# Hymba-style trunk step on one core: weight splits between normed blocks, operand of the output projection rounded in parts, modulation group 35 moved, root table earlier, last stores from two queues

## The reference, cut to what matters

```
mod = silu(c) @ ada_w + ada_b                      # 9 vectors of 2048: shift, scale, gate of three parts
x += 0.5 * g1 * SwiGLU_1(RMSNorm(x) * (1 + s1) + b1)        # 2048 -> 5504 -> 2048
h  = RMSNorm(x) * (1 + s2) + b2
[xb | yb | q | k | v] = h @ w_in                            # 28 blocks of 128 columns
lru = RG-LRU(conv4(xb)) * gelu(yb)                          # 8 heads of 128
att = window attention with sinks(rope(q), rope(k), v)      # 8 q heads, 2 kv heads
x += g2 * ([lru | att] @ w_out)
x += 0.5 * g3 * SwiGLU_2(RMSNorm(x) * (1 + s3) + b3)
y = RMSNorm(x) * norm_final
```

## Time and profile before

| | us |
|---|---|
| median of 3 runs | 2408.03 (2407.75 to 2410.68) |
| profiled execution, its own time | 2407.99 |
| span of its profile | 2405.5 |
| TensorE busy | 2356.3 (98%) |
| VectorE busy | 1202.7 (50%) |
| ScalarE busy | 838.0 (35%) |
| GpSimd busy | 151.1 (6%) |
| mean granted clock of TensorE | 0.995 |

### The profile page before, as it was taken

The page is one execution under the profiler, slowest core; times in us unless marked ns, Lnnn a source line. Parts: engine busy times, 40 slices in busy tenths (PEclk is TensorE's granted clock), DMA queues, the critical chain, the costliest instruction groups (busy, mean ns, idle before and its releaser), DMA issues.

```text
span 2405.5 us, 45693 instructions
## 1 busy us (share of the span) xinstructions
PE 2356.3 (98%) x17264; PEld 2258.3 (94%) x17264; DVE 1202.7 (50%) x2084; ACT 838.0 (35%) x1130; POOL 151.1 (6%) x176
## 2 busy tenths in 40 slices
PE   7999999999999999998999998999999999999998
PEld 3888999999999999998999898999999999999998
DVE  3665434434533454357676746454454454456344
ACT  3332222222222232334566634332333232333234
POOL 3000000000000000021031211000000000000003
PEclk9999999999999999999999999999999999999999
DMA  9999998889889948863444453554554555454553
GB/s 316 359 332 350 281 278 266 263 262 278 270 258 278 270 147 245 255 192 114 146 134 123 123 148 116 147 157 138 154 157 140 149 156 148 140 159 147 145 154 104
DMA packets 680252, 480.98 MB, mean 200 GB/s; under 512 B 15349, under 2 KB 603785, under 8 KB 679801
## 3 DMA queue, kind: packets, MB, share of 16 engines
q1 hardware_dynamic: 678224, 473.36, 65.8%
q0 software_dynamic: 1776, 6.26, 0.8%
q10 hardware_dynamic: 162, 0.14, 0.0%
HBM read 476.53 MB, written 5.13 MB: 200 GB/s over the span
## 4 chain that ended last, share of the span: by engine, by line
PE 91%; DVE 4%; ACT 2%; issue 1%; DMA 1%; DVEq 0%; ACTq 0%
PE ps L558 28%; PE ps L560 28%; PE ps L559 28%; PE ps L569 6%; PE ps L544 1%; DVE lo L1366 1%; DMA ident<-in_identity 0%; ACT hi L1021 0%; DMA mod_raw<-in_ada_w 0%; DVE work L1679 0%; DVE h_lo L1412 0%; DVE work L1725 0%; DVE work L1681 0%; DVE work L1401 0%; DVE work L1427 0%
## 5 line engine op out<-in xcount | busy, mean ns | idle before, releaser
L558 PE MATMUL ps<-h_hi,hi 128*128 128x320 f32 x3456 | 1079.0, 312 | 18.5 <-DVE h_lo L1412 11.8
L560 PE MATMUL ps<-h_hi,lo 128*128 128x320 f32 x3456 | 1070.5, 310 | 0.0
L559 PE MATMUL ps<-h_lo,hi 128*128 128x320 f32 x3456 | 1070.5, 310 | 0.0
L1366 DVE TENSOR_TENSOR lo<-raw,hi 128x1024 fp32r<-128x1024 f32 (+1 forms) x608 | 731.8, 1221 | 492.3 <-ACT hi L1021 491.1
L1021 ACT ACTIVATE hi<-raw 128x1024 fp32r<-128x1024 f32 (+1 forms) x608 | 624.9, 1050 | 1009.6 <-PE ps L560 875.9
L558 PEld LDWEIGHTS ps<-h_hi,hi 128*128 128x128 f32 x3456 | 651.3, 188 | 35.2 <-issue 28.4
L559 PEld LDWEIGHTS ps<-h_lo,hi 128*128 128x128 f32 x3456 | 651.4, 188 | 0.7
L560 PEld LDWEIGHTS ps<-h_hi,lo 128*128 128x128 f32 x3456 | 651.2, 188 | 0.0
L558 PE MATMUL ps<-a_hi,hi 128*128 128x320 f32 x1376 | 426.8, 310 | 1.3 <-DVE a_lo L1540 1.3
L560 PE MATMUL ps<-a_hi,lo 128*128 128x320 f32 x1376 | 425.2, 309 | 0.0
L559 PE MATMUL ps<-a_lo,hi 128*128 128x320 f32 x1376 | 425.1, 309 | 0.0
(11 more groups left out here) (221 smaller groups left out, 875.5 us busy)
## 6 DMA issues: line engine op xcount, KB each, us to landing
raw<-in_ffn_w_gate SPq DMA_DIRECT2D x172, 512.0 KB, 4.2
raw<-in_ffn_w_up SPq DMA_DIRECT2D x172, 512.0 KB, 5.1
raw<-in_ffn_w_down SPq DMA_DIRECT2D x160, 512.0 KB, 4.8
mod_raw<-in_ada_w SPq DMA_DIRECT2D x144, 512.0 KB, 7.8
work<-in_ada_w SPq DMA_DIRECT2D x144, 512.0 KB, 8.2
raw<-in_w_in SPq DMA_DIRECT2D x56, 512.0 KB, 3.8
raw<-in_w_out SPq DMA_DIRECT2D x32, 512.0 KB, 3.8
raw<-in_ffn_w_down SPq DMA_DIRECT2D x16, 384.0 KB, 2.9
```

Source lines behind the costliest of these rows:

```text
L558: mm(out, w_hi, r_hi, start=first, stop=False)
L559: mm(out, w_hi, r_lo, start=False, stop=False)
L560: return mm(out, w_lo, r_hi, start=False, stop=last)
L1366: v.tensor_tensor(lo_slot(u)[:, 0:n], raw_slot(u)[:, 0:n], hi_slot(u)[:, 0:n], ALU.subtract).then_inc(lo_done, 1)
```

## The change

1. `modulate` for the mixer's norm and for the second SwiGLU's norm does the splits of units 4 and 5 itself, ahead of blocks 11 and 13 (`EARLY`); the loops that follow start at their third unit.
2. Group 35: parts 0 and 1 stand between the two matmuls of `sum_of_squares(1)`, parts 2 to 7 behind them; `copy_group(35)` stands between the root and `modulate`, `mod_turn(35)` and `add_mod(35)` behind the mixer's first four projections.
3. `root_table` (the throw-away root) is taken out of `rms`, and out of the program's end, and stands behind the square of block 14.
4. End of the mixer: blocks 0 to 6 are rounded ahead of the last projection's end (`early_operand`), blocks 8 to 11 before the last attention job, 12 to 15 after it; the splits of the output projection's units 4 to 6 stand between what is left of head 7's work.
5. The one store of the last column group that ScalarE's copy feeds is issued from ScalarE's queue (11 stores are left to SyncE).

```diff
+EARLY = (11, 13)
...
+                    if q == 3 and who == "A":
+                        continue
...
                     pe.wait_ge(summed, SUMMED[n] + KB - 1)
                     mm(psum[:, B_NORM, 0:T], ones, sum_sq, start=True, stop=False)
+                    for part in range(first_parts):
+                        mod_unit(part, 35)
                     pe.wait_ge(squared, n * KB + KB)
                     mm(psum[:, B_NORM, 0:T], ones, sq[:, (KB - 1) % 2, :], start=False, stop=True).then_inc(ms_ready, 1)
...
-                    down_eight(u, 0, g, 0, a0 + 4 * CB + TAIL, 35)
+                    down_eight(u, 0, g, 0, a0 + 4 * CB + TAIL, None)
...
-            sum_of_squares(1)
+            sum_of_squares(1, 2)
+            for part in range(2, MODS):
+                mod_unit(part, 35)
...
+                if kv == 0:
+                    pe.wait_ge(mod_done, 36)
...
             four_blocks(U_MIX, (first[0:2], first[2:4]), KB)
+            mod_turn(35)
...
+            def root_table():
+                run(warm, eps, ACT.Sqrt)
+
             def rms(n):
-
-                run(warm, eps, ACT.Sqrt)
...
                 for k in range(first, end):
+                    if u is not None and k in EARLY:
+                        finished(u + EARLY.index(k))
+                        split(u + EARLY.index(k) + SPLIT)
...
+                        if n == KB - 2:
+                            root_table()
...
-            modulate(1, 3, 0, KB)
+            copy_group(35)
+            modulate(1, 3, 0, KB, U_MIX)
...
+            def early_operand():
+
+                act.wait_ge(lru_done, LH - 1)
+                for k in range(LH - 1):
+                    run(h_hi[:, k, :], mix[:, k, :], ACT.Copy).then_inc(early_hi, 1)
...
                         act.wait_ge(o_copied, 12)
-                        operand(LH, KB)
+                        operand(LH + GRP, KB)
...
             for n in range(4, MIX_BLOCKS):
                 finished(U_MIX + 2 * n)
                 split(U_MIX + 2 * n + SPLIT)
+                if n == MIX_BLOCKS - 1:
+                    early_operand()
                 finished(U_MIX + 2 * n + 1)
                 evacuate(n)
+                if n == MIX_BLOCKS - 1:
+                    act.wait_ge(o_copied, 6)
+                    operand(LH, LH + GRP)
                 behind(n)
                 split(U_MIX + 2 * n + 1 + SPLIT)
                 if MIX_KIND[n][0] == "y" and n < MIX_BLOCKS - 1:
                     gate_functions(*MIX_KIND[n][1:], n)
 
+            finished(U_OUT)
+            split(U_OUT + SPLIT)
             gate_functions(NKV - 1, GRP - 1, MIX_BLOCKS - 1)
-            operand(0, LH)
+            for n in range(1, 3):
+                finished(U_OUT + n)
+                split(U_OUT + n + SPLIT)
+            act.wait_ge(lru_done, LH)
+            run(h_hi[:, LH - 1, :], mix[:, LH - 1, :], ACT.Copy).then_inc(h_hi_ready, LH)
...
-            with act.Fori(0, 4) as i:
+            for n in range(3, 8):
+                finished(U_OUT + n)
+                split(U_OUT + n + SPLIT)
+                if n >= 4:
+                    square(n - 4, 2, x_done, X_OUT + n - 3)
...
+                        if m == 2:
+                            root_table()
...
             ffn(U_F2, G_F2, X_F2, 3, False)
-            run(warm, eps, ACT.Sqrt)
...
+                        if q == 3:
+                            act.wait_ge(y_copied, Y_DONE[q, t][1])
+                            act.dma_start(y_rows(q, t), y_tok[0:rows, t, 4 * q * P:4 * (q + 1) * P]).then_inc(stored, 16)
...
                 for k in range(first, end + 2):
+                    if u is not None and k - 1 in EARLY:
+                        finished(u + EARLY.index(k - 1))
+                        split(u + EARLY.index(k - 1) + SPLIT)
...
+            add_mod(35)
...
                 behind(n)
-                if n == MIX_BLOCKS - 1:
-                    operand(LH, KB)
+                if last:
+                    operand(LH, LH + GRP)
+                    split(U_MIX + 2 * n + SPLIT)
+                    operand(LH + GRP, KB)
                 split(U_MIX + 2 * n + 1 + SPLIT)
                 if MIX_KIND[n][0] == "y" and n < MIX_BLOCKS - 1:
                     recurrence(GRP * MIX_KIND[n][1] + MIX_KIND[n][2])
 
             operand(0, LH - 1)
+            finished(U_OUT)
+            split(U_OUT + SPLIT)
             recurrence(LH - 1)
             operand(LH - 1, LH)
...
-            with dve.Fori(0, 4) as i:
+            for n in range(1, 8):
+                finished(U_OUT + n)
+                if n >= 4:
+                    update(n - 4, G_OUT + n - 4, 5, G_OUT + n - 4 - ACT_FREED)
+                split(U_OUT + n + SPLIT)
```

More of the change, by code:

```diff
@@ L1162, in ffn @@
                         up_pair(u, i * 2, g, i + 31)
-                    last_down(u + CB * 4, 35)
+                    last_down(u + CB * 4, None)
                 else:
-                    for n in range(8):
+                    for n in range(len(EARLY), 8):
                         finished(u0 + n)
@@ L1427, in reciprocal, with modulate @@
                 v.reciprocal(rstd, rms_t).then_inc(rstd_ready, 1)
-            def modulate(n, sc, sh, first, end):
+            def modulate(n, sc, sh, first, end, u=None):
                 if n:
@@ L1791, in _ @@
                     evacuate(1)
+            add_mod(35)
             pick_sinks()
             for n in range(4, MIX_BLOCKS):
+                last = n == MIX_BLOCKS - 1
                 finished(U_MIX + 2 * n)
-                split(U_MIX + 2 * n + SPLIT)
+                if not last:
+                    split(U_MIX + 2 * n + SPLIT)
                 finished(U_MIX + 2 * n + 1)
```

40 lines of the change are left out of this document (23 added, 17 removed).

## The result

| | before | after |
|---|---|---|
| median, us | 2408.86 (2407.75 to 2410.68, 4 runs) | 2394.06 (2393.35 to 2395.99, 4 runs) |
| profiled execution, us | 2407.99 | 2393.35 |
| its span, us | 2405.5 | 2391.6 |

The ratio is 0.9937, with a 95% interval of 0.9925 to 0.9949: faster by 14.8 us. The forecast was 2395.4 us.

The account below looks back on a forecast made before the run. TensorE, busy 98% of the span, was taken to bound the kernel. The terms 3.6 + 0.5 + 2.4 + 3.9 + 1.5 + 0.7 = 12.6 us took 2407.99 to 2395.4 us, range 2392.8 to 2398.5 us.

Parts of the forecast that it names:

- Group 35: Its 32 matmuls move into the gap of the mixer's norm, where TensorE waits anyway: 3.6 us saved (3.1 to 3.6).
- The root's table: In the mixer's norm the root starts as L610 ends, 0.5 us earlier; in the second norm nothing is won.
- Early splits: TensorE's waits for unit 4 in the mixer and second SwiGLU go: 1.4 + 1.0 = 2.4 us saved, 0 at least.
- The clock in the mixer's norm: Rows do not decide whether it falls after the new 3 us gap; nothing counted, 1.5 us kept for the range.
- the first rival: The clock holds in the mixer's norm too, 1.5 us more saved: 2393.9 us, chance 0.25.
- The mixer's end: TensorE's waits after its last values and at the output projection's unit 4 go: 1.7 + 2.2 = 3.9 us (2.2 to 3.9).
- 1.5 for the clock: At the mixer's end the clock stays at full speed instead of falling for 3.4 us: 1.5 us saved (0 to 1.5).
- block 12: At the mixer's end VectorE reaches it just in time for TensorE; 0 to 0.3 us of wait may be left.
- The end: At the program's end the early table saves 0.7 us (0.7 to 1.3); the second store queue saves 0.
- a new wait: Rival: block 11 or 12, or head 7's gate functions, come late in the early splits' place: 2398.8 us, chance 0.08.
- no gain at the mixer's end: Rival: another wait, hidden so far, ends as late there; 3.9 and 1.5 us are lost: 2400.8 us, chance 0.04.
- a clock that stays low: Rival: after the mixer's norm the clock stays low through dense products; at 40 us of it 2413 us, chance 0.02.

Follow-up runs that it names:

- experiments 1: The changed kernel with group 35 back beside the down projection, ahead of the last 16 units: 2399.42 us, ratio 0.9958 to the kernel before.
- 12: The changed kernel with group 34 in the mixer's norm, group 35 and state turns in the second norm, VectorE's old order at the mixer's end: 2388.73 us.
- experiment 4: The changed kernel with the root's table loaded where it was before the change: 2396.40 us, ratio 0.9946 to the kernel before.
- experiment 2: The changed kernel without the early splits between the normed blocks: 2398.70 us, ratio 0.9957 to the kernel before.
- experiment 3: The changed kernel with the mixer's end as before (rounding, remainders, splits and loops of both engines): 2400.44 us, ratio 0.9963 to the kernel before.
- Experiment 5: The changed kernel with the output projection's units 4 to 6 split behind all of head 7 again: 2394.71 us, ratio 0.9936 to the kernel before.
- experiments 8: The changed kernel with VectorE making all eight attention blocks before it splits the output projection's unit 2: 2393.13 us, ratio 0.9929 to the kernel before.
- 10: The changed kernel with VectorE's old order at the mixer's end, GpSimd's last-head products held until VectorE's first four remainders are made: 2393.50 us, ratio 0.9935.
- experiment 9: The changed kernel once more, unedited: 2393.96 us, ratio 0.9935 to the kernel before.
- experiments 7: The changed kernel plus 24 modulation-shaped matmuls with unused results in the second norm's gap: 2392.96 us, ratio 0.9931 to the kernel before.

## Why the prediction was right, point by point

The sum gave 12.6 us less than the profiled execution of before; it is 14.6 us less (2407.99 to 2393.35), and the medians differ by 14.8.

- **Group 35:** 3.6 us forecast, 3.58 measured. The stage scatters by 1.3 us from profile to profile, so that close an agreement is luck; experiments 1 and 12 give 4.4 us each. Both margins held, the matmuls of parts 0 and 1 within the wait for the last square, and the row's copy by 0.1 us.
- **The root's table:** 0.5 us forecast, 0.51 measured, and 0.51 given back in experiment 4. In the second norm 0, as forecast (8.27 and 8.27).
- **Early splits:** the waits of 1.35 and 1.02 us are gone and no block came late, as forecast. But the step "Saved 1.4 + 1.0 = 2.4 us" took the wait for the whole price. In the mixer it is that only while the clock falls: 1.40 us from the kernel before to the profiles with a fall (237.23 to 235.83), 2.81 us to the changed kernel's, and 1.6 and 3.05 us by experiment 2. The reading is that a wait behind a chain of fixed length hides the clock's fall, and that removing the wait exposes what the clock does; the mixer's norm has no run with late splits and a held clock that would show it there. In the second SwiGLU experiment 2 gives 1.98 us.
- **The clock in the mixer's norm:** this is where the single number missed. "I count nothing, and keep 1.5 us for the range" chose the fall. In both profiles of the changed kernel the clock held, which was the first rival, 2393.9 us at a chance of 0.25; its size is right (1.42 us), and so is its time (2393.35 and 2394.06). Over the kernels with that gap the two outcomes came six and five times, so neither should have been left out of the middle of the range. As far as these runs show, which of the two came with this kernel was luck.
- **The mixer's end:** 3.9 us for the two waits and 1.5 for the clock, 5.4 in all, forecast; 1.90 + 3.13 = 5.03 measured. The clock stayed, as forecast. The missing part is block 12: "just covered, 0 to 0.3 us may be left" became 0.59 us, since "four blocks (0.4 us each, taken like ScalarE's 2.99 / 8)" was wrong for VectorE beside GpSimd, where the four took 2.62 us. The second wait and the clock have no prices of their own: experiment 3 shows that they share one distance of 18.04 us, so that the clock's 1.5 us could be saved only together with the late split. The sum took both and came out right. Experiment 5 shows that with the early rounding this split is late by only 0.66 us.
- **The end:** 0.7 us forecast, 0.60 measured (0.65 at the root). Experiment 4 gives back 0.64 us at the root and 0.29 at the end, a stretch that took 14.1 to 14.5 us in the other eleven profiles with the early table. The second queue gave 0, as forecast, at a DMA share of 0.97 to 0.98.
- **Not in the sum:** the second SwiGLU gained 1.62 us where 1.0 was forecast. Products ran at the low clock for 4.2 us behind its norm, and for 5.0 us in the kernel before, which is worth 0.4 us at 0.45 us each; the other 0.2 us are open. This stretch differs from profile to profile (911.1 to 912.4 us for the stage in the ten profiles that are alike there).

The rivals with a new wait (0.08), with no gain at the mixer's end (0.04) and with a clock that stays low (0.02) did not come. Of the first there is a trace, the 0.59 us.

## What to carry to other kernels

A wait behind a chain of fixed length on another engine hides slower work ahead of it, as at the mixer's end: take the distance between two anchors in both traces, not the wait alone, to price its removal. Work that an engine must do anyway is free in a gap in which it waits, and it may also shorten that gap enough for its clock to hold; here two groups of modulation products gave 3.6 us each for the move and up to 1.9 us for the clock. Price an elementwise instruction by rows in which the same neighbours run, since four subtractions of VectorE took half as long again with GpSimd's products beside the first two.

## What was unexpected of the hardware

- **VectorE beside GpSimd.** Four subtractions of 128x320 took 1.70 us alone and 2.62 us with two products of GpSimd on blocks of 128x320 beside the first two, and the first of those products took 0.47 us alone and 1.19 us beside VectorE (experiments 8 and 10 differ only in when GpSimd begins).
- **The clock behind a gap is not settled by the gap's length.** A gap of 1.74 us was followed by the low clock in the kernel before and not in experiment 3. Gaps of 2.9 us were passed over six times and not five times in the mixer's norm. The gaps of 3.42 us (once) and of 5.64 us (always) brought it down.
- **The fall keeps its own time.** In all eight profiles in which the clock fell at the mixer's norm it did so 1051.3 us after it had risen at the start, whatever the edit (experiment 9). That this decides whether a gap of 2.9 us is passed over is not shown.
- **The clock held behind products with 32 columns of weights.** The modulation's products in the gap of experiments 7 and 12 ran at a granted clock of 1.00, and the 2.91 and 2.48 us of idleness behind them did not bring it down; it is one profile of each.
